# A hybrid decoder layer on one core: the fourth expert's down projection by column quarters, stores between them, and the last group of experts loaded in 4 MB transfers

## The chip, the cores and the metric

The kernel runs on one core of a Trainium2 chip. The metric is the device time of one execution in microseconds (us), the median of several. A profiled execution gives the trace from which the rows below come; its span runs from the first to the last instruction.

## What is computed

One step of one decoder layer, in fp32, for a prompt of 256 tokens and 8 sample tokens (264 rows of width 2048). First the mixer (differential attention and a short convolution side by side); then the part that this change touches, a mixture of 32 SwiGLU experts in 4 routing groups:

```python
def expert_block(args):
    xblk, e = args
    return (jax.nn.silu(xblk @ w_gate[e]) * (xblk @ w_up[e])) @ w_down[e]
...
xp = xp + hier_moe(rms_norm(xp, norm_ffn[l]), ...)   # top 1 group, top 2 experts in it
```

Each of the three matrices of an expert is 2048 x 512 or 512 x 2048 in fp32: 4 MB. All 32 experts are read, 96 matrices or 403 MB. Outputs are y_prompt (256 x 2048), y_sample (8 x 2048) and the keys, values and convolution states.

## The kernel before

**Stages.** Up to some 530 us the mixer and the router run. Then follow the experts, in 8 groups (NG) of 4 (EG). An expert has 32 slots (C) for tokens; 4 experts make up the 128 columns of a selection matrix.

**Names.** g, u and d with a digit are the gate, up and down matrix of an expert in a group (0 to 3). A matrix fills two of the 8 slots of `ring`, 2 MB each (a unit). SP issues all weight transfers in the order of LOADS: g0 u0 g1 u1 d0 g2 u2 d1 g3 u3 d2 d3. A transfer is issued once the unit that it overwrites has been used (`expert_used`). Groups 1 to 6 are loaded by `pairs`, one 4 MB transfer for a matrix; the first and the last group in units of 2 MB (line 539), the very last unit in two halves of 1 MB (lines 610 and 611).

**TensorE, expert by expert.** `gather` picks an expert's tokens, `turn_rows` turns them; `unit_products` (line 981) multiply them with g and u, four matmuls of 32 columns side by side, each giving a quarter of the contraction; `fold` adds the four parts up. `turn_hidden` turns the hidden rows and `down` (line 1018) multiplies them with d. `down` works through the contraction (4 chunks c, two in a unit) and in each chunk through the 4 column quarters n, which accumulate side by side in the 4 strips of 32 rows of bank 2. ScalarE copies bank 2 to `ye`: row strip n holds the expert's 32 slots for columns 512n to 512n+511. Software order puts `down` of expert j - 1 behind the products of expert j, and `mix` of expert j - 2 in between.

**Mix.** `turn_gate` (line 1049) turns the gate matrix (tokens x slots) into `gateT`, four times, one copy in each strip of 32 partitions. `mix` then multiplies 32 rows of `gateT` with 32 rows of `ye`, for each quarter n and row block t: t = 0 and 1 are the prompt's two blocks of 128 tokens, t = 2 the 8 sample tokens (line 1033, a 32x32 tile; the others line 1036). VectorE adds the result from its bank to `xa` (lines 1830 and 1824).

**The group's end.** Behind the products of the fourth expert (j = 3): four products `residual` (line 1055) load `xa[:, 1]` into banks 0, 1, 3 and 4, on which `mix_row` (line 1060) accumulates both last experts for row block 1; ScalarE moves the banks back to `xa` (line 1425). `mix_part` (line 1042) mixes the third expert for row block 0. Then gate 3 is turned, `down(3, 0)` and `down(3, 1)` run back to back, ScalarE copies `ye`, and the last expert is mixed: row block 0, row block 1, samples.

**Stores.** After the last group SP stores row block 0 in four transfers of 256 KB (line 624) and the samples in four of 16 KB (line 627), ScalarE's queue stores row block 1 in four of 256 KB (line 1437).

Of the kernel before, what the change touches and what calls it, by code (L numbers as in the profile page):

```python
# [15 lines left out]
ALU = mybir.AluOpType  # L16
# [103 lines left out]
STEPS = [(t, j) for j in range(EG - 2) for t in (0, 2, 1)] + [(t, j) for j in (EG - 2, EG - 1) for t in (0, 2)]  # L120
NSTEPS = len(STEPS) + 1
STEP_AT = {s: n + (n > STEPS.index((0, EG - 2))) for n, s in enumerate(STEPS)}
# [5 lines left out]
MIX_BANKS = {s: (4, 5, 6, 7) for s in STEPS}  # L128
MIX_BANKS.update({(2, j): (2,) for j in range(EG)})
MIX_BANKS[(0, EG - 2)] = (5, 7, 6, 5)  # L130
MIX_BANKS[(2, EG - 2)] = (7,)
MIX_BANKS[(0, EG - 1)] = (5, 6, 7, 2)
MIX_BANKS[(2, EG - 1)] = (5,)
ROW_BANKS = (0, 1, 3, 4)
GATE_BANK = (5, 5, 5, 6)
# [27 lines left out]
def build(nc, ins, outs):  # L163
    ctx = ExitStack()
    with ctx:
# [107 lines left out]
        gateT = bc[:, y0 + 2816:y0 + 3200].rearrange("p (t s) -> p t s", t=TT)  # L273
        g_sb = bc[:, y0 + 3200:y0 + 3712]
# [159 lines left out]
        end_in = sem("end_in")  # L434
# [5 lines left out]
        row_mixed = sem("row_mixed")  # L440
# [41 lines left out]
        def _(sp):  # L482
# [67 lines left out]
            def pairs(g, it):  # L550

                for n in range(UPG // 2):
                    kind, j = LOADS[n]
                    s = slot_of(NFRONT + TURN + 2 * n)
                    if 2 * n < SLOTS:
                        expert_used(2 * n + 1 - SLOTS + UPG, it - 1)
                    else:
                        expert_used(2 * n + 1 - SLOTS, it)
                    src = {"g": wg, "u": wu, "d": wd}[kind][bass.ds(g, 1), :, j, :].rearrange("o p n -> p (o n)")
                    sp.dma_start(ring[:, s:s + 2, :].rearrange("p a n -> p (a n)"), src).then_inc(slot_full[s], 16)  # L560
                    sp.sem_inc(slot_full[s + 1], 16)
                sp.sem_inc(end_in, 16)
# [25 lines left out]
            sp.sem_inc(end_in, 16)  # L588
# [10 lines left out]
            with sp.Else():  # L599
                for m in range(UPG):  # L600
                    s = slot_of(NFRONT + TURN + m)
                    if m < SLOTS:
                        expert_used(m - SLOTS + UPG, NG - 2)
                    else:
                        expert_used(m - SLOTS, NG - 1)
# [7 lines left out]
            y = outs["y_prompt"].rearrange("o (t p) d -> (o t) p d", p=P)  # L613
            every = npass * (NG * NADDS)
            last = EG - 1

            def added(step, n):

                sp.wait_ge(mix_added, every + (ADDS_BY[step] + n))

            for n in range(4):
                added((0, last), n - 3)
                cols = slice(512 * n, 512 * n + 512)
                sp.dma_start(y[0][:, cols], xa[:, 0, cols]).then_inc(y_stored, 16)
            added((2, last), 0)
            for n in range(4):
                sp.dma_start(outs["y_sample"].rearrange("b o d -> b (o d)")[:, n * 512:(n + 1) * 512],
                             xa[n * C:n * C + NB, 2, 0:512]).then_inc(y_stored, 16)
            sp.wait_ge(y_stored, 192)
# [6 lines left out]
        def _(pe):  # L636
# [265 lines left out]
            def gather(j, it):  # L902

                if j == 0:
                    pe.wait_ge(sel_ready, it + 5)
                elif j == 1:
                    pe.wait_ge(sel_ready, it + 4)
                    pe.wait_ge(mix_added, it * NADDS + NADDS)
# [42 lines left out]
            def experts(it, first):  # L951
# [49 lines left out]
                def down(j, i, hidden_of=None):  # L1001
# [9 lines left out]
                    for c in range(FC // 2):  # L1011
                        if (j, i, c) == (EG - 1, 1, 1):
                            pe.wait_ge(end_in, it * 16 + 16)
# [25 lines left out]
                def mix_part(step, n):  # L1039

                    rows_ = slice(n * C, (n + 1) * C)
                    return pe.matmul(bank[MIX_BANKS[step][n]][:, :], gateT[rows_, step[0], :], ye[rows_, :], start=True, stop=True)

                def turn_gate(j):

                    to = bank[GATE_BANK[j]]
# [6 lines left out]
                def residual(n):  # L1053

                    pe.matmul(bank[ROW_BANKS[n]][:, :], ident, xa[:, 1, n * 512:(n + 1) * 512], start=True, stop=False)  # L1055

                def mix_row(j, n):

                    rows_ = slice(n * C, (n + 1) * C)
                    m = pe.matmul(bank[ROW_BANKS[n]][:, :], gateT[rows_, 1, :], ye[rows_, :], start=False, stop=j == EG - 1)  # L1060
                    if j == EG - 1:
                        m.then_inc(row_mixed, 1)

                def next_rows(j):

                    if j == 0:
                        pe.wait_ge(mix_added, it * NADDS + NADDS)
                        pe.wait_ge(row_moved, it * 4 + 4)
                    gather((j + 1) % EG, it)

                for j in range(EG):
# [3 lines left out]
                    if j == 0:  # L1075
                        pe.wait_ge(row_moved, it * 4 + 2)
# [6 lines left out]
                    else:  # L1083
# [4 lines left out]
                        else:  # L1088
                            pe.wait_ge(ye_copied, e - 1)
# [33 lines left out]
                    if j == EG - 1:  # L1123
                        residual(2)
                    down(j - 1, 1)

                e = it * EG + EG - 1
                pe.wait_ge(xe_ready, 2 * e + 4)
                pe.wait_ge(ye_copied, e)
                pe.wait_ge(gateT_copied, e)  # L1130
                mix_part((0, EG - 2), 0)
                mix_part((0, EG - 2), 1)
                pe.wait_ge(act_ready, e + 1)
                mix_part((0, EG - 2), 2).then_inc(mixed, 1)
                for n in range(4):
                    mix_row(EG - 2, n)
                adds_done((0, EG - 2), -2)
                mix_part((0, EG - 2), 3).then_inc(mixed, 1)
                mix((2, EG - 2))
                adds_done((0, EG - 2), -1)  # L1140
                turn_gate(EG - 1)
                down(EG - 1, 0)
                down(EG - 1, 1)
                pe.wait_ge(ye_copied, e + 1)
                pe.wait_ge(gateT_copied, e + 1)
                adds_done((2, EG - 2))
                mix((0, EG - 1))
                for n in range(4):
                    if n == 3:
                        adds_done((0, EG - 1), -3)  # L1150
                    mix_row(EG - 1, n)
                mix((2, EG - 1))
# [9 lines left out]
        def _(act):  # L1162
# [228 lines left out]
            def experts(it, first):  # L1391

                def copy_gate(e, j):

                    act.wait_ge(gate_T, e + 1)
                    A(gateT, bank[GATE_BANK[j]][:, 0:TT * P].rearrange("p (t s) -> p t s", t=TT), ACT.Copy).then_inc(gateT_copied, 1)
# [6 lines left out]
                for j in range(EG):  # L1403
# [8 lines left out]
                    if j == 0:  # L1412
                        copy_gate(e, j)
                        continue
                    copy_ye(e - 1)
# [5 lines left out]
                copy_gate(it * EG + EG - 1, EG - 1)  # L1421
                copy_ye(it * EG + EG - 1)
                for n in range(4):
                    act.wait_ge(row_mixed, it * 4 + (n + 1))
                    A(xa[:, 1, n * 512:(n + 1) * 512], bank[ROW_BANKS[n]][:, :], ACT.Copy).then_inc(row_moved, 1)
# [8 lines left out]
            for n in range(4):  # L1434
                cols = slice(512 * n, 512 * n + 512)
                act.wait_ge(row_moved, npass * (NG * 4) + (n + 1))
                act.dma_start(y[1][:, cols], xa[:, 1, cols]).then_inc(y_stored, 16)
# [3 lines left out]
        def _(dve):  # L1441
# [343 lines left out]
            V.memset(esum[:, 2:3], 0.0).then_inc(row_moved, 4)  # L1785
# [14 lines left out]
            with dve.Fori(0, npass) as r:  # L1800
                with dve.Fori(0, NG) as g:
# [16 lines left out]
                    def mix_adds(step):  # L1818
# [7 lines left out]
                        for n in range(4):  # L1826
                            if step == (0, EG - 2) and n == 3:
                                dve.wait_ge(mixed, it * NSTEPS + (NSTEPS + STEP_AT[step] + 2))
# [3 lines left out]
                    for j in range(EG):  # L1832
# [5 lines left out]
                        if j >= 2:  # L1838
                            for t in (0, 2, 1):
                                if (t, j) == (1, 2):  # L1840
                                    dve.wait_ge(row_moved, it * 4 + 4)
# [10 lines left out]
                    for t in (0, 2):  # L1852
                        mix_adds((t, EG - 2))
                    for t in (0, 2):
                        mix_adds((t, EG - 1))
# [109 lines left out]
```

## Time and profile before

| | us |
|---|---|
| median of 3 runs | 1441.41 (1439.46 to 1441.7) |
| profiled execution, its own time | 1440.47 |
| its span, first to last instruction | 1438.6 |
| TensorE busy | 1256.8 (87%) |
| VectorE busy | 450.5 (31%) |
| ScalarE busy | 223.1 (16%) |
| moved by DMA | 503.61 MB, mean 350 GB/s |
| mean granted TensorE clock | 0.959 |

The profiled execution's own time lies 1.9 us above its span. Busy shares are averages over stages with different limits; only waits in a stage tell what sets its pace. A row of the form `[5.01 <-DMA x]` says that the engine stood 5.01 us before this instruction and that the DMA x ended the wait. An fp32 matmul appears as two instructions (x2). Four matmuls that run side by side in strips overlap, so that their group's busy time is short.

### The profile page before, as it was taken

The page shows a single profiled execution, that of the slowest core. Times are in us where ns is not written, and L with a number is a line of the kernel's source. Part 1 is how long each engine was busy: PE and PEld are TensorE (multiplying, and loading weights), DVE is VectorE, ACT ScalarE, POOL GpSimd, SP SyncE. Part 2 cuts the span into 40 slices and gives each one's busy share as a digit, 9 for nine tenths or more (in the row PEclk, how much of TensorE's full clock was granted, in tenths as well). Part 3 has the DMA queues.
Part 4 walks back from the last instruction along what each step waited for, and adds up shares of the span by engine and source line. Part 5 has one row for each costly group of instructions (what it writes and reads, how often), then busy time and mean ns, then how long its engine had stood idle before and what let it go on. Part 6 is the DMA issues. An engine that isn't in the chain of part 4 may idle for free.

```text
span 1438.6 us, 19986 instructions
## 1 busy us (share of the span) xinstructions
PE 1256.8 (87%) x8413; PEld 650.3 (45%) x8413; DVE 450.5 (31%) x887; ACT 223.1 (16%) x465; POOL 44.8 (3%) x30
## 2 busy tenths in 40 slices
PE   8999999999999998997787777887788777778777
PEld 7888888888788862231222222222222122222222
DVE  4322127674211142332321321331232232233142
ACT  3111232322000033110011011011001001111101
POOL 0000003140000001000000000000000000000000
PEclk9999999999999999999998999899899999999899
DMA  9975443669399349999999999999999999999997
GB/s 342 348 222 183 141 132 121 207 203 340 89 349 409 119 164 428 417 428 430 433 428 436 427 433 436 427 434 431 430 436 427 433 436 426 436 428 426 430 429 308
DMA packets 101729, 503.61 MB, mean 350 GB/s; under 512 B 9470, under 2 KB 79750, under 8 KB 85302
## 3 DMA queue, kind: packets, MB, share of 16 engines
q1 hardware_dynamic: 89618, 494.37, 84.6%
q10 hardware_dynamic: 12068, 8.63, 1.9%
q8 instruction: 32, 0.52, 0.1%
q14 instruction: 11, 0.09, 0.0%
HBM read 496.42 MB, written 6.59 MB: 350 GB/s over the span
## 4 chain that ended last, share of the span: by engine, by line
PE 55%; DMA 41%; DVE 2%; ACT 1%; issue 1%; SPq 1%; ACTq 0%; DVEq 0%
PE bank L702 30%; DMA ring<-in_w_gate 16%; DMA ring<-in_w_up 14%; DMA ring<-in_w_down 10%; PE bank L981 9%; PE bank L1018 4%; PE bank L916 2%; PE bank L1036 2%; DMA ring<-in_w_in 1%; PE bank L1033 1%; PE bank L1055 1%; DVE xa L1830 1%; PE bank L1049 1%; PE bank L998 0%; PE bank L793 0%
## 5 line engine op out<-in xcount | busy, mean ns | idle before, releaser
L702 PE MATMUL bank<-bc,ring 128*128 128x264 f32 x1536 | 350.9, 387 | 1.9 <-ACT cat L1186 1.3
L981 PE MATMUL bank<-ring,bc 128*32 128x512 f32 x2040 | 268.2, 659 | 89.5 <-DMA ring<-in_w_gate 58.5
L702 PEld LDWEIGHTS bank<-bc,ring 128*128 128x128 f32 x1536 | 288.1, 190 | 52.4 <-issue 2.3
L1830 DVE TENSOR_TENSOR xa<-xa,bank 128x512 f32<-128x512 f32 x192 | 119.8, 682 | 243.5 <-PE bank L1036 196.0
L981 PEld LDWEIGHTS bank<-ring,bc 128*32 128x32 f32 x2040 | 63.2, 117 | 264.5 <-issue 153.4
L702 PE MATMUL bank<-cat,ring 128*128 128x264 f32 x512 | 116.0, 387 | 0.0
L702 PEld LDWEIGHTS bank<-cat,ring 128*128 128x128 f32 x512 | 96.6, 190 | 19.0 <-issue 2.9
L1844 DVE COPY bc<-bank 128x512 f32<-128x512 f32 x32 | 22.1, 691 | 210.3 <-PE bank L981 210.3
L1018 PE MATMUL bank<-ring,cat 128*32 128x512 f32 x480 | 66.4, 674 | 19.9 <-DMA ring<-in_w_down 19.7
L916 PE MATMUL bank<-cat,bc 128*32 128x512 f32 x512 | 61.3, 597 | 13.5 <-DVE xa L1830 13.5
L1018 PE MATMUL bank<-ring,xa 128*32 128x512 f32 x512 | 62.3, 607 | 6.3 <-DMA ring<-in_w_down 4.1
L1406 ACT ACTIVATE bc<-bank 128x512 f32<-128x512 f32 x32 | 19.1, 596 | 264.4 <-PE bank L981 264.4
L1036 PE MATMUL bank<-bc 32*128 32x512 f32 x320 | 51.5, 716 | 8.0 <-ACT bc L1401 6.3
L1498 DVE RECIPROCAL xa<-xa 128x264 f32<-128x264 f32 x16 | 28.8, 1803 | 85.2 <-ACT xa L1236 85.2
L991 PE MATMUL bank<-bc,consts 128*32 128x512 f32 x64 | 32.8, 593 | 21.7 <-DVE bc L1844 21.7
L1401 ACT ACTIVATE bc<-bank 128x512 f32<-128x512 f32 x32 | 19.1, 597 | 195.8 <-PE bank L1018 195.8
L1875 POOL TENSOR_TENSOR ring<-ring 128x1024 f32<-128x1024 f32 x16 | 37.6, 2376 | 285.1 <-DVE xa L1547 285.1
L1765 DVE TENSOR_TENSOR bc<-bank,gains 128x512 f32<-128x512 f32 x32 | 22.1, 692 | 74.4 <-PE bank L923 74.4
L1018 PEld LDWEIGHTS bank<-ring,cat 128*32 128x32 f32 x480 | 13.4, 117 | 56.0 <-issue 35.3
L1373 ACT ACTIVATE bc<-bank 128x512 f32<-128x512 f32 x32 | 19.1, 597 | 124.5 <-PE bank L916 124.5
L1678 DVE TENSOR_TENSOR bc<-bc,bank 128x264 f32<-128x264 f32 x16 | 6.9, 429 | 99.4 <-PE bank L702 99.4
L1036 PEld LDWEIGHTS bank<-bc 32*128 32x128 f32 x320 | 14.4, 211 | 51.7 <-issue 34.9
(286 smaller groups left out, 981.9 us busy)
## 6 DMA issues: line engine op xcount, KB each, us to landing
ring<-in_w_gate SPq DMA_DIRECT2D x24, 4096.0 KB, 31.2
ring<-in_w_up SPq DMA_DIRECT2D x24, 4096.0 KB, 31.3
ring<-in_w_down SPq DMA_DIRECT2D x24, 4096.0 KB, 32.6
ring<-in_w_in SPq DMA_DIRECT2D x23, 2048.0 KB, 13.9
ring<-in_w_up SPq DMA_DIRECT2D x16, 2048.0 KB, 22.9
ring<-in_w_gate SPq DMA_DIRECT2D x15, 2048.0 KB, 28.9
ring<-in_w_down SPq DMA_DIRECT2D x13, 2048.0 KB, 28.7
ring<-in_w_out SPq DMA_DIRECT2D x8, 2048.0 KB, 16.5
```

What stands on the lines that cost most here:

```text
L702: m = pe.matmul(bank[n % 3][:, 0:T], w[:, k, (i % TPU) * P:(i % TPU + 1) * P], src[:, k, :], start=n_k == 0, stop=n_k == KT - 1)
L916: m = pe.matmul(bank[4][c * C:(c + 1) * C, :], lhs, rhs, start=t == 0, stop=t == TT - 1, skip_group_check=True)
L981: m = pe.matmul(bank[b][c * C:(c + 1) * C, :], xeT[j % 2][:, k, :], wx, start=i == 0 and x < 4, stop=i == 1 and x >= 4, skip_group_check=True)
L991: pe.matmul(bank[3][0:C, :], const("fold"), g_sb, start=True, stop=True, skip_group_check=True)
L1018: m = pe.matmul(bank[2][n * C:(n + 1) * C, :], actT[j % 2][:, i * FC // 2 + c, :], wc[:, n * 512:(n + 1) * 512], start=i == 0 and c == 0, ...
L1036: m = pe.matmul(bank[to[n]][:, :], gateT[rows_, t, :], ye[rows_, :], start=True, stop=True)
L1373: A(xrow, bank[4][:, :], ACT.Copy).then_inc(xrow_copied, 1)
L1498: st.do(V.reciprocal(r, r))
L1765: V.tensor_tensor(xeT[j % 2].rearrange("p (m c) s -> p m c s", m=4), bank[7][:, :].rearrange("p (m c s) -> p m c s", m=4, c=4), gffn.rearr ...
L1830: V.tensor_tensor(xa[:, t, cols], xa[:, t, cols], bank[to[n]][:, :], ALU.add).then_inc(mix_added, 1)
L1844: V.tensor_copy(u_sb, bank[1][:, :]).then_inc(u_copied, 1)
L1875: G.tensor_tensor(kp, kp, ring[:, sq_, (b % 4) * ATT:(b % 4 + 1) * ATT], ALU.mult).then_inc(page_mul, 1)
```

## The change

1. In the last group each matrix is one 4 MB transfer. The last one, d3, comes in three: columns 0 to 1023 of all chunks (2 MB), then quarters 2 and 3 (1 MB each), with a semaphore of their own.
2. In all groups the fourth expert's `down` goes by column quarters: `end_products(q)` runs the 4 contraction chunks of quarter q side by side in the strips of bank 2, each a part sum. ScalarE copies the bank to `g_sb` or `u_sb` in turn.
3. The sum over the chunks is left to the mix: `mix_last(q)` multiplies all 128 rows of a gate matrix of its own, `gateT3` (four equal copies of the gates), with the 128 rows of part sums. It accumulates on what `mix_second_last` put into the same bank for the third expert.
4. Gate 3 is turned before `down(2)` instead of before `down(3)`; three of the four `residual` products go, one stays, for quarter 3 of row block 1. VectorE does the other adds of row block 1.
5. The stores go by column quarter: row blocks 0 and 1 together (512 KB) and the samples for quarters 0 to 2, each as soon as its adds are done; for quarter 3 samples and row block 0 on SP, row block 1 on ScalarE's queue.

```diff
+END_STEPS = [(t, q) for q in range(3) for t in (0, 1, 2)] + [(t, 3) for t in (2, 0, 1)]
+END_BANKS = {0: (5, 0, 3, 5), 1: (7, 1, 4, 7), 2: (6, 6, 6, 6)}
...
-                for m in range(UPG):
-                    s = slot_of(NFRONT + TURN + m)
...
-                    if m < UPG - 1:
-                        stream_unit(NG - 1, m, s)
-                        continue
-                    src = source(NG - 1, m)
-                    sp.dma_start(ring[:, s, 0:UNIT // 2], src[:, 0:UNIT // 2]).then_inc(slot_full[s], 16)
-                    sp.dma_start(ring[:, s, UNIT // 2:], src[:, UNIT // 2:]).then_inc(end_in, 16)
+                for n in range(UPG // 2):
+                    kind, j = LOADS[n]
+                    s = slot_of(NFRONT + TURN + 2 * n)
...
+                    if n < UPG // 2 - 1:
+                        src = {"g": wg, "u": wu, "d": wd}[kind][NG - 1, :, j, :]
+                        sp.dma_start(ring[:, s:s + 2, :].rearrange("p a n -> p (a n)"), src).then_inc(slot_full[s], 16)
+                        sp.sem_inc(slot_full[s + 1], 16)
+                        continue
+                    src = wd[NG - 1, :, EG - 1, :].rearrange("p (c d) -> p c d", c=FC)
+                    to = ring[:, s:s + 2, :].rearrange("p a (c d) -> p (a c) d", c=FC // 2)
+                    sp.dma_start(to[:, :, 0:1024], src[:, :, 0:1024]).then_inc(slot_full[s], 16)
+                    sp.sem_inc(slot_full[s + 1], 16)
+                    for q in (2, 3):
+                        cols = slice(512 * q, 512 * q + 512)
+                        sp.dma_start(to[:, :, cols], src[:, :, cols]).then_inc(end_in[q - 2], 16)
...
+            for q in range(3):
+                cols = slice(512 * q, 512 * q + 512)
+                sp.wait_ge(end_added, every + END_ADD[(1, q)])
+                sp.dma_start(y[:, :, cols], xa[:, 0:2, cols]).then_inc(y_stored, 16)
+                sp.wait_ge(end_added, every + END_ADD[(2, q)])
+                sp.dma_start(ys[:, cols], xa[q * C:q * C + NB, 2, 0:512]).then_inc(y_stored, 16)
...
+                def mix_second_last(t, q):
+
+                    rows_ = slice(q * C, (q + 1) * C)
+                    pe.matmul(bank[END_BANKS[t][q]][:, :], gateT[rows_, t, :], ye[rows_, :],
+                              start=(t, q) != (1, 3), stop=False, skip_group_check=True)
+
+                def end_products(q):
+
+                    if q == 0:
+                        pe.wait_ge(ye_copied, it * (EG - 1) + EG - 1)
...
+                    else:
+                        pe.wait_ge(end_copied, it * 4 + q)
+                    if q >= 2:
+                        pe.wait_ge(end_in[q - 2], it * 16 + 16)
+                    for c in range(FC):
+                        m = pe.matmul(bank[2][c * C:(c + 1) * C, :], actT[(EG - 1) % 2][:, c, :],
+                                      end_weights[c // 2][:, c % 2, q * 512:(q + 1) * 512], start=True, stop=True, skip_group_check=True)
...
+                def mix_last(q):
+
+                    pe.wait_ge(end_copied, it * 4 + q + 1)
+                    for t, q_ in END_STEPS:
+                        if q_ != q:
+                            continue
+                        if t == 2:
+                            m = pe.matmul(bank[END_BANKS[2][q]][q * C:(q + 1) * C, :], gateT3[:, 2, 0:C], (g_sb, u_sb)[q % 2],
+                                          start=False, stop=True, skip_group_check=True)
+                        else:
+                            m = pe.matmul(bank[END_BANKS[t][q]][:, :], gateT3[:, t, :], (g_sb, u_sb)[q % 2],
+                                          start=False, stop=True, skip_group_check=True)
+                        m.then_inc(end_mixed, 1)
...
                     if j == EG - 1:
-                        residual(0)
-                        residual(1)
-                        residual(3)
+                        pe.wait_ge(gateT_copied, e)
+                        turn_gate(EG - 1)
...
-                    if j == EG - 1:
-                        residual(2)
                     down(j - 1, 1)
...
+                pe.wait_ge(act_ready, e + 1)
+                end_products(0)
...
+                for t in (0, 1):
+                    for q in range(3):
+                        mix_second_last(t, q)
+                for q in range(4):
...
+                end_products(1)
+                mix_last(0)
+                end_products(2)
+                mix_last(1)
...
+                pe.matmul(bank[END_BANKS[1][3]][:, :], ident, xa[:, 1, 1536:2048], start=True, stop=False, skip_group_check=True)
+                mix_second_last(1, 3)
+                mix_second_last(0, 3)
+                end_products(3)
+                mix_last(2)
+                mix_last(3)
```

## Rows read from the trace of the kernel before

**Rows 1.** The page: 40 slices of TensorE and DMA rate, and the chain by engine.
```profile
PE   8999999999999998997787777887788777778777
...
GB/s 342 348 222 183 141 132 121 207 203 340 89 349 409 119 164 428 417 428 430 433 428 436 427 433 436 427 434 431 430 436 427 433 436 426 436 428 426 430 429 308
...
PE 55%; DMA 41%; DVE 2%; ACT 1%; issue 1%; SPq 1%; ACTq 0%; DVEq 0%
```

**Rows 2.** Windows: length, busy us (instructions) by engine, granted clock, DMA share, GB/s.
```profile
12.00:30.00 18.00, 16.11 (x72) 13.35 (x73) 8.93 (x30) 5.37 (x11) 0.00 (x0) 1.00 1.07 366
...
700.00:1300.00 600.00, 477.16 (x3772) 137.87 (x3765) 163.76 (x312) 69.94 (x124) 0.00 (x0) 0.93 1.00 432
1310.00:1418.00 108.00, 89.37 (x714) 25.46 (x714) 29.98 (x58) 12.94 (x23) 0.00 (x0) 0.94 1.01 429
...
1424.00:1426.00 2.00, 2.00 (x32) 0.74 (x25) 0.23 (x1) 0.49 (x1) 0.00 (x0) 1.00 0.11 45
```

**Rows 3.** Issue to landing: all of line 560 (4 MB), then line 611 (last megabyte).
```profile
DMA to landing us min/median/max: 21.8/31.4/35.1
...
L611 SPq DMA_DIRECT2D ring<-in_w_down x1: 433/433/433, 1389.8 to 1389.8; - x1
...
DMA to landing us min/median/max: 35.5/35.5/35.5
```

**Rows 4.** Timeline of TensorE, groups 1, 5, 6, 7: first products with g3, first L1042.
```profile
695.78 3.64 PE L981 MATMUL bank<-ring,bc 128*32 128x512 f32 x16 [5.15 <-DMA ring<-in_w_gate]
...
724.30 0.70 PE L1042 MATMUL bank<-bc 32*128 32x512 f32 x3 [0.76 <-issue]
...
1162.08 3.27 PE L981 MATMUL bank<-ring,bc 128*32 128x512 f32 x16 [5.07 <-DMA ring<-in_w_gate]
...
1278.65 3.64 PE L981 MATMUL bank<-ring,bc 128*32 128x512 f32 x16 [5.01 <-DMA ring<-in_w_gate]
...
1307.51 0.70 PE L1042 MATMUL bank<-bc 32*128 32x512 f32 x3 [0.76 <-issue]
...
1395.99 1.92 PE L981 MATMUL bank<-ring,bc 128*32 128x512 f32 x16 [1.00 <-DMA ring<-in_w_gate]
...
1418.85 0.70 PE L1042 MATMUL bank<-bc 32*128 32x512 f32 x3 [0.76 <-issue]
```

**Rows 5.** Windows: the first products with g3 in group 6.
```profile
1278.60:1282.30 3.70, 3.65 (x20) 0.68 (x20) 0.00 (x0) 0.00 (x0) 0.00 (x0) 0.50 1.00 427
```

**Rows 6.** The chain that ended last, from 1410 us: start, us, what.
```profile
1410.15 2.58 PE bank L1055 x6
...
1415.17 1.06 PE bank L1055 x2
1416.23 1.85 PE bank L1018 x16
1418.08 0.76 issue
...
1422.49 0.99 PE bank L1033 x8
1423.48 0.79 PE bank L1049 x24
...
1427.77 0.60 ACT bc L1401
...
1428.50 1.14 PE bank L1036 x8
...
1432.62 0.69 DVE xa L1824
```

**Rows 7.** The stores: SP's issues (timeline), and the window in which bytes begin.
```profile
1430.41 2.13 SPq L624 DMA_DIRECT2D out_y_prompt<-xa  x4
...
1433.34 3.28 SPq L627 DMA_DIRECT2D out_y_sample<-xa  x4
...
1431.00:1431.50 0.50, 0.50 (x4) 0.01 (x2) 0.50 (x1) 0.50 (x3) 0.00 (x0) 1.00 0.46 176
```

More of the change, by code:

```diff
@@ L115 @@
 SLOPES = [2.0 ** (-8.0 * (h + 1) / H) for h in range(H)]
[L120 to L122 removed]
+STEPS = [(t, j) for j in range(EG - 2) for t in (0, 2, 1)]
+NSTEPS = len(STEPS)
+STEP_AT = {s: n for n, s in enumerate(STEPS)}
 ADDS_BY, _n = {}, 0
@@ L433, in build @@
         half_used = sem("half_used")
-        end_in = sem("end_in")
+        end_in = [sem(f"end_in{i}") for i in range(2)]
         down_half = sem("down_half")
@@ L613, in _ @@
[L613 to L628, printed above, removed]
@@ L630, in _ @@
+            cols = slice(1536, 2048)
+            sp.wait_ge(end_added, every + END_ADD[(2, 3)])
+            sp.dma_start(ys[:, cols], xa[3 * C:3 * C + NB, 2, 0:512]).then_inc(y_stored, 16)
+            sp.wait_ge(end_added, every + END_ADD[(0, 3)])
+            sp.dma_start(y[:, 0, cols], xa[:, 0, cols]).then_inc(y_stored, 16)
+            sp.wait_ge(y_stored, 144)
             sp.wait_ge(state_stored, 16)
@@ L1037, in mix @@
                     m.then_inc(mixed, 1)
-                def mix_part(step, n):
-                    rows_ = slice(n * C, (n + 1) * C)
-                    return pe.matmul(bank[MIX_BANKS[step][n]][:, :], gateT[rows_, step[0], :], ye[rows_, :], start=True, stop=True)
                 def turn_gate(j):
-                    to = bank[GATE_BANK[j]]
+                    to = bank[5]
                     for t in range(TT):
@@ L1414, in experts @@
                         continue
+                    if j == EG - 1:
+                        copy_gate(e, j)
                     copy_ye(e - 1)
@@ L1420, in experts @@
                               ).then_inc(x0_ready, 1)
[L1421 to L1425, printed above, removed]
+                for q in range(4):
+                    if q < 3:
+                        act.wait_ge(end_down, it * 3 + q + 1)
+                    else:
+                        act.wait_ge(down_done, it * EG + EG)
+                    if q >= 2:
+                        act.wait_ge(end_mixed, it * len(END_MIX) + 3 * (q - 1))
+                    A((g_sb, u_sb)[q % 2], bank[2][:, :], ACT.Copy).then_inc(end_copied, 1)
+                act.wait_ge(end_mixed, it * len(END_MIX) + END_MIX[(1, 3)])
+                A(xa[:, 1, 1536:2048], bank[END_BANKS[1][3]][:, :], ACT.Copy).then_inc(row_moved, 1)
             experts(0, True)
@@ L1433, in _ @@
             y = outs["y_prompt"].rearrange("o (t p) d -> (o t) p d", p=P)
[L1434 to L1437, printed above, removed]
+            act.wait_ge(row_moved, npass * NG + 1)
+            act.dma_start(y[1][:, 1536:2048], xa[:, 1, 1536:2048]).then_inc(y_stored, 16)
         @block.vector
@@ L1851, in _ @@
                             select(0, P, False)
[L1852 to L1855, printed above, removed]
+                    for t, q in END_ADD:
+                        dve.wait_ge(end_mixed, it * len(END_MIX) + END_MIX[(t, q)])
+                        rows_ = slice(q * C, (q + 1) * C) if t == 2 else slice(0, P)
+                        cols = slice(0, 512) if t == 2 else slice(q * 512, (q + 1) * 512)
+                        V.tensor_tensor(xa[rows_, t, cols], xa[rows_, t, cols], bank[END_BANKS[t][q]][rows_, :], ALU.add
+                                        ).then_inc(end_added, 1)
             assert st.n - before == LOOP_STEPS, st.n - before
```

97 lines of the change are left out of this document (39 added, 58 removed).

## The prediction

> **What bounds the kernel now.** I read the 40 slices first. From 540 us to the last slice the DMA moves 417 to 436 GB/s, in all but one 426 or more, while TensorE is busy seven or eight tenths in most slices [rows 1]. The chain gives TensorE 55% and the DMA 41% of the whole, but in the expert stage what TensorE waits for last is a weight transfer. So two questions decide: does the stream stay full, and what stands between the last weights and the end?
>
> The stream: 432 GB/s from 700 to 1300 us, where each transfer is 4 MB and the DMA engines' busy share is 1.00, and 429 GB/s from 1310 to 1418 us, where the last group comes in 2 MB [rows 2]. Issues land 31.4 us later in the median, 21.8 at least [rows 3]. One 4 MB transfer takes 9.71 us of the stream: TensorE starts on the fourth expert's gate matrix ("g3") the moment it lands, at 1162.08 and 1278.65 us, 116.57 us or 12 transfers apart, and at 695.78 four groups before 1162.08 (116.58 us each) [rows 4]. So at issue there are always 12 us or more of other bytes queued ahead. That is the cover of everything that TensorE does later in groups 0 to 6.
>
> The end: the last megabyte is issued at 1389.8 and landed 35.5 us later, 1425.3 us [rows 3]; bytes have nearly stopped in 1424 to 1426 us [rows 2]. TensorE isn't waiting for it: it is still at the group's tail, a chain without a gap above 0.8 us from 1410 to the end of the last mix at 1432.6 us [rows 6]. Then come one add (0.69 us), four stores of the sample rows that hold SP for 3.28 us, and 2.0 us from the last issue (1436.6) to the end, 1438.6 us [rows 6, 7]. So the end is set by TensorE's chain behind the gate and up matrices of the fourth expert, and 6.0 us of adds and stores behind it.
>
> **Part 1: 4 MB transfers in the last group.** Gain: with 12 transfers in the group's rhythm g3 is whole at 1278.60 + 116.57 = 1395.2 us, where its second half now lands at 1396.0 [rows 4]; 0.8 us. Loss: now its first half is there at 1391.0, and TensorE does eight products, two mixes and their adds before the second half comes; the first mix of the third expert (L1042) starts at 1418.85, 22.9 us after the second half [rows 4]. With a whole pair, groups 1 to 6 show the same work: 28.5, 28.3, 27.8, 27.8, 27.5 and 28.9 us from g3's arrival to that mix, mean 28.1 (the first and the last of the six are shown) [rows 4]. The long ones are those in which the first 16 instructions after 5 us of idling took 3.64 us, where at 1395.99, after 1 us of waiting, they took 1.92: the granted clock was 0.50 in that stretch [rows 5], the level of 1.2 GHz, after TensorE had stood for 5 us. I take 28.1: the mix would start at 1395.2 + 28.1 = 1423.3 us instead of 1418.85. This costs 4.4 us, the biggest term. The issues themselves wait for the later half of what they overwrite, some microseconds more; they have 12 us of queue ahead and cost nothing. The other weights keep pace: u3 at 1404.9 and d2 at 1414.6 us, against a first `down` of expert 2 at 1415.3 below.
>
> **Part 2: residual products and the gate transposes moved.** The four products that put row block 1 into the banks go (2.58 + 1.06 us), and the transposes of gate 3 come to their place (0.79 us) [rows 6]: -2.85 us. They cover the wait for the hidden product less than the residuals did; 0.79 us just reach it, a miss costs some 0.1 to 0.4 us. So the fourth expert's first quarter can start at 1423.3 - 2.85 = 1420.4 us. Its wait for `ye` is the same 0.76 us as now [rows 6].
>
> **Part 3: the last matrix in pieces.** It would land whole at 1395.2 + 3 x 9.71 = 1424.3 us, its first two column quarters 4.9 us sooner, 1419.4. Pieces are 4 KB and 2 KB instead of 8 KB and more. The nearest row is the window 12 to 30 us with w_in's 1 KB pieces: 366 GB/s against 432 [rows 2], so 2.87 us instead of 2.43 for a megabyte of 1024 pieces, 0.43 ns a piece. 512 pieces of 4 KB and 1024 of 2 KB cost 0.7 us together: first half 1419.6, last 1425.0 us. Bounds: 0 and twice that. The Trainium skill (DMA: Bandwidth & Descriptors, Specifications) says that pieces of 512 B or more run at line rate; by that the 0.7 us are nothing, the row speaks against it, and the sum is the same either way. For TensorE is at quarter 0 at 1420.4, and at quarter 3 only ten microseconds later: the landing no longer sets anything, by 0.8 us at the first quarter.
>
> **Part 4: the new tail on TensorE.** The unit is one round of the array with 512 columns in fp32, 0.86 us: L1055's three full matmuls take 2.58 us; four matmuls of 32 columns or of 32 rows side by side take the same round plus a change of tiling: L1018 1.85 for two rounds (+0.13), L1033 0.99 (+0.13), L1036 1.14 (+0.28), a single full one 1.06 (+0.20) [rows 6]. No row has a 128-row, 32-column matmul alone; it can't be under a round, and at most two of them share one.
> - `end_products`, 4 calls: 4 rounds, as many as `down` had.
> - `mix_second_last` for quarters 0 to 2: 2 rounds; both of quarter 3 use the same 32 rows: 2 rounds.
> - the sample rows' second-last mixes: 1 round.
> - `mix_last`: row blocks 0 and 1 take a full matmul for each quarter: 8 rounds. Now they are 1.14 us for four.
> - sample rows: 4 matmuls of 32 columns, the last two side by side: 3 rounds.
> - one residual product: 1 round.
>
> 21 rounds are 18.1 us. Changes of tiling: six to 32-column form at 0.13, two to 32-row form at 0.28, one to 32x32 at 0.13, five to full at 0.20: 2.5 us. Sum 20.5 us; bounds 18.1 (no change costs anything) and 21.4 (the last two sample mixes one by one). The Trainium skill (TensorEngine Tiling, Key Properties) has the rule that speaks against this change: switching the tiling form drains the engine. It names no price; the trace agrees with 0.13 to 0.28 us where the form changes and 0.00 within L1055's three. Without the rule the sum would be 2.5 us less.
>
> Every other wait in the tail is covered: ScalarE's copy of a quarter (0.60 us [rows 6]) lies under 1 to 3 rounds, VectorE's 11 adds (0.69 each) come one for each round. TensorE ends at 1420.4 + 20.5 = 1440.9 us, now 1432.6.
>
> **Part 5: the stores.** Now 6.0 us from TensorE's end. The last product is (row block 1, quarter 3); behind it ScalarE's copy 0.6, its issue 0.4, 2.0 from the last issue to the end as now [rows 7], 256 KB more to move at 379 GB/s or so 0.7, and 0.2 of hops: 3.9 us. The six stores of quarters 0 to 2 have gone under the tail. Bounds 3.1 (the first store's bytes begin 0.9 us after its issue [rows 7], so part of the 2.0 may be shared) and 4.9 (the quarter-2 store of 512 KB and two sample stores of 0.8 us each on SP still ahead).
>
> **Part 6: groups 0 to 6.** The same tail there, some 4 us longer, and d3's slots free about 5 us later, since TensorE must await d3 whole (1307.7 us in group 6) before the first quarter. Behind it are only queue entries with 12 us of other bytes ahead [rows 3], and TensorE, however late its tail, stands 5 us before g3 of the next group [rows 4]. Nothing, and the full price of a dry queue if 12 us weren't enough.
>
> **Sum.** 1440.9 + 3.9 = 1444.8 us of span, against 1438.6: +6.2 (4.4 from Part 1, -2.85 from Part 2, +6.7 for the tail (20.5 against 13.8 from 1418.85 to 1432.6), -2.1 from the stores). The profiled execution took 1440.47 us for its span of 1438.6, 0.9 under the median. 1440.5 + 6.2 = 1446.7 and 1441.4 + 6.2 = 1447.6; I forecast 1447.0.
>
> **Rivals.**
> *A, as summed* (0.60): 1447.0, its own range 1444.5 to 1449.5.
> *B, not slower by what can be told* (0.17): the new tail packs better than counted. For: matmuls of 32 rows and 32 columns overlap in these rows down to one round for four, and the sample mixes and the next `end_products` have the same form. If three sample rounds vanish and half the changes cost nothing, the tail is 20.5 - 2.6 - 1.2 = 16.7 us, and the time 1443.2. It decides from 3.3 us saved on (0.2% is 2.9). Against: in each pair one 32-column strip is shared, and full products lie between.
> *C, faster* (0.07): the full mixes take one pass of 0.43 instead of two. 8 x 0.43 = 3.4 saved wouldn't do; it needs every round of the tail near half: 1437.5. L1055's rows, same form and type, speak against it.
> *D, slower still* (0.12): after the 6 us wait for g3 the lower clock lasts longer, or the stores queue: 1450.
> *E* (0.04): a dry queue in the middle groups, 2 us for each of seven groups or more: 1455 or beyond.
>
> If Part 1 doesn't bite (full clock after g3's wait), the landing at 1419.6 us is next, so it gives back only 0.8 us; that stays in A.
>
> **Range and chances.** A measurement of this kernel can tell about 0.2% (2.9 us) from no change. The range goes from B's lower side, 1441.5, to D, 1450.5. Slower: A, D, E and none of B, 0.76; within 0.2%: B, 0.17; faster 0.07.
>
> **What would show it.** In the profile after: g3 in group 7 waited for until 1395.2 and first `end_products` near 1420.4; no DMA wait at quarters 1 to 3; full mixes of 0.86 us each in `mix_last`; TensorE's last product near 1441; the ACT-queue store as the last thing, some 4 us behind it; 432 GB/s unchanged from 700 to 1300 us. The prediction is wrong if the tail from first quarter to last product is under 17 us, or if g3's chain takes under 25 us.

## The result, and the profile after

The changed kernel takes 1447.24 us in the median of six executions, the kernel before, measured with it, 1440.77: ratio 1.0039 (95% interval 1.0028 to 1.005), so it is slower. One of the six took 2173.69 us at a mean granted clock of 0.553; the ratio leaves it out, and the median of the other five is 1446.86 us, 6.1 us over the kernel before. The forecast was 1447.0. The profiled execution took 1447.63 us for a span of 1445.5.

The page after: DMA rate in 40 slices and the chain by engine.

```profile
GB/s 342 348 223 181 136 131 124 216 192 345 100 347 388 117 196 428 394 434 432 429 428 435 433 431 428 434 435 429 428 434 435 430 429 433 435 430 431 431 434 228
...
PE 65%; DMA 30%; DVE 2%; ACT 1%; issue 1%; SPq 1%; ACTq 0%; DVEq 0%
```

The stream is as full as before from the eighteenth slice on; the 17th lost 23 GB/s, and the last is emptier, since more work stands behind the last weights. TensorE has 10 points more of the chain. Most of them lie in the middle groups, where the chain now meets mainly the down matrices (25% of the span; before it was gate 16%, up 14%, down 10%). In the last group the chain leaves the DMA for good at g3's landing (1396.3 us), where before it left it at u3's (1405.6), which is some 9 us. Windows, columns as in [rows 2]: the middle of the stage, then the first products with g3 in the last group.

```profile
700.00:1300.00 600.00, 496.54 (x3758) 142.88 (x3761) 168.67 (x316) 71.56 (x124) 0.00 (x0) 0.93 1.00 432
...
1396.30:1400.00 3.70, 3.70 (x20) 0.72 (x20) 0.00 (x0) 0.00 (x0) 0.00 (x0) 0.50 1.01 434
```

432 GB/s, unchanged, though TensorE works 19 us more in the 600: the longer tails of groups 0 to 6 are hidden. The answers to [rows 3]: issue to landing of all of line 562 (the 4 MB transfers in the loop), then the first half of d3 and its quarter 3.

```profile
DMA to landing us min/median/max: 17.9/31.1/34.3
...
DMA to landing us min/median/max: 29.7/29.7/29.7
...
L622 SPq DMA_DIRECT2D ring<-in_w_down x1: 17689/17689/17689, 1392.5 to 1392.5; - x1
...
DMA to landing us min/median/max: 33.6/33.6/33.6
```

The shortest time to landing fell from 21.8 to 17.9 us, about what the group's end grew by (6.7 us of tail less 2.85 before it); with 9.7 us for a transfer's own bytes, 8 us of queue are left. The first half of d3 was issued at 1391.1 and landed at 1420.8, quarter 3 at 1426.1. TensorE's chain through the last group (start, us, what):

```profile
1396.30 3.64 PE bank L990 x16
...
1421.05 0.61 ACT bc L1424
1421.65 0.04 issue
1421.70 1.06 PE bank L1071 x8
1422.76 1.92 PE bank L1058 x12
1424.68 0.99 PE bank L1162 x8
1425.67 1.00 PE bank L1071 x8
1426.67 1.91 PE bank L1087 x4
1428.58 0.55 PE bank L1084
1429.13 0.03 PE bank L1071 x3
1429.16 0.40 PE bank L1084
1429.56 0.86 PE bank L1071 x5
...
1433.31 1.05 PE bank L1169 x2
1434.36 1.91 PE bank L1058 x4
1436.28 0.99 PE bank L1071 x8
...
1439.18 0.98 PE bank L1084 x4
1440.17 1.93 PE bank L1087 x4
```

L1071 is `end_products`, L1058 `mix_second_last`, L1087 the full `mix_last`, L1084 its 32-column form, L1169 the residual product. From the first quarter at 1421.70 to the end of the last product at 1442.10 TensorE doesn't wait once. Two full matmuls take 1.91 us each time: two rounds of 0.86 and 0.2 for the change of tiling. At 1428.58 the sample mix and the next `end_products` are interleaved, and four strips with five matmuls take two rounds. Behind it, timeline of the last stores:

```profile
1441.63 0.29 SPq L635 DMA_DIRECT2D out_y_sample<-xa  x1
1442.12 0.60 ACT L1455 ACTIVATE xa<-bank 128x512 f32<-128x512 f32 x1 [4.08 <-PE bank L1087]
1442.35 0.36 SPq L637 DMA_DIRECT2D out_y_prompt<-xa  x1
1442.74 0.37 ACTq L1465 DMA_DIRECT2D out_y_prompt<-xa  x1
```

The last store is issued 0.6 us after the last product, and the span ends 2.4 us after that issue ends: 3.4 us from TensorE's end, where it was 6.0.

### The profile page after: what moved, and what is told of

The parts are those of the page before. It is cut to its first block, busy times and chain, and to the rows that moved or that the text cites. A ratio compares the mean times of both kernels' runs of the same rounds, so it can differ in the third digit from the quotient of the medians.

```text
span 1445.5 us, 20006 instructions
## 1 busy us (share of the span) xinstructions
PE 1292.9 (89%) x8365; PEld 658.6 (46%) x8365; DVE 459.6 (32%) x896; ACT 225.7 (16%) x465; POOL 44.8 (3%) x30
## 4 chain that ended last, share of the span: by engine, by line
PE 65%; DMA 30%; DVE 2%; ACT 1%; issue 1%; SPq 1%; ACTq 0%; DVEq 0%
PE bank L711 30%; DMA ring<-in_w_down 25%; PE bank L990 9%; DMA ring<-in_w_gate 4%; PE bank L1087 4%; PE bank L925 4%; PE bank L1025 3%; PE bank L1058 3%; PE bank L1071 3%; PE bank L1084 2%; DMA ring<-in_w_in 1%; PE bank L1000 1%; PE bank L1162 1%; PE bank L1007 1%; PE bank L1169 1%
## 5 line engine op out<-in xcount | busy, mean ns | idle before, releaser
L990 PE MATMUL bank<-ring,bc 128*32 128x512 f32 x2040 | 253.4, 631 | 62.7 <-DMA ring<-in_w_gate 60.9
L1857 DVE TENSOR_TENSOR xa<-xa,bank 128x512 f32<-128x512 f32 x128 | 79.4, 682 | 149.0 <-PE bank L1043 142.7
L1883 DVE TENSOR_TENSOR xa<-xa,bank 128x512 f32<-128x512 f32 (+1 forms) x88 | 60.4, 686 | 164.5 <-PE bank L1087 157.1
L1071 PE MATMUL bank<-ring,xa 128*32 128x512 f32 x256 | 46.7, 702 | 29.6 <-DMA ring<-in_w_down 28.1
L1025 PE MATMUL bank<-ring,cat 128*32 128x512 f32 x480 | 59.5, 599 | 4.5 <-DVE bc L1874 2.9
L1087 PE MATMUL bank<-bc,xa 128*128 128x512 f32 x128 | 63.5, 618 | 0.0
L1429 ACT ACTIVATE bc<-bank 128x512 f32<-128x512 f32 x32 | 19.1, 596 | 221.5 <-PE bank L990 221.5
L1453 ACT ACTIVATE bc<-bank 128x512 f32<-128x512 f32 x32 | 19.1, 597 | 153.9 <-PE bank L1071 153.9
L1043 PE MATMUL bank<-bc 32*128 32x512 f32 x256 | 40.8, 710 | 1.7 <-DVE xa L1857 1.7
L1025 PE MATMUL bank<-ring,xa 128*32 128x512 f32 x256 | 33.3, 627 | 9.2 <-DMA ring<-in_w_down 8.4
L1087 PEld LDWEIGHTS bank<-bc,xa 128*128 128x128 f32 x128 | 21.7, 189 | 43.2 <-issue 43.2
```

Source lines behind the costliest of these rows:

```text
L990: m = pe.matmul(bank[b][c * C:(c + 1) * C, :], xeT[j % 2][:, k, :], wx, start=i == 0 and x < 4, stop=i == 1 and x >= 4, skip_group_check=True)
L1025: m = pe.matmul(bank[2][n * C:(n + 1) * C, :], actT[j % 2][:, i * FC // 2 + c, :], wc[:, n * 512:(n + 1) * 512], start=i == 0 and c == 0, ...
L1043: m = pe.matmul(bank[to[n]][:, :], gateT[rows_, t, :], ye[rows_, :], start=True, stop=True)
L1071: m = pe.matmul(bank[2][c * C:(c + 1) * C, :], actT[(EG - 1) % 2][:, c, :], end_weights[c // 2][:, c % 2, q * 512:(q + 1) * 512], start=Tr ...
L1087: m = pe.matmul(bank[END_BANKS[t][q]][:, :], gateT3[:, t, :], (g_sb, u_sb)[q % 2], start=False, stop=True, skip_group_check=True)
L1857: V.tensor_tensor(xa[:, t, cols], xa[:, t, cols], bank[to[n]][:, :], ALU.add).then_inc(mix_added, 1)
```

## The experiments

Theory: three terms make the time. (1) A pair that lands whole delays the chain behind g3. (2) The last expert's tail is TensorE work, round by round. (3) Stores between take bytes from the end. Rival: only one of them counts and the others are hidden. Each kernel was timed in alternation with the kernel before; the ratio is to that.

**The changed kernel again.** 

> The changed kernel once more, for comparison on the same chip: 6.4 us over the kernel before. If the first group's short gap in the weight stream (1.1 us more than in the profile of before) belongs to the change and not to one execution, it is there again at 580 to 585 us.

1446.41 us, 1.0039 (1.0025 to 1.0052). The gap in the stream was there too. Where it comes from is below.

**Term 1 alone.**

```diff
-                for m in range(UPG):
+                for n in range(11):
+                    kind, j = LOADS[n]
...
+                    sp.dma_start(ring[:, s:s + 2, :].rearrange("p a n -> p (a n)"), src).then_inc(slot_full[s], 16)
+                    sp.sem_inc(slot_full[s + 1], 16)
+                for m in range(22, UPG):
```

> The kernel before with only its last group's loads changed: g0 to d2 in 4 MB transfers, d3 as before. Theory (the products with g3 now begin when the whole pair has landed): g3 at 1395.2, the first mix of the third expert 27.5 to 28.9 us later at 1423.3 instead of 1418.85, the tail of 13.8 us and the 6.0 us behind it unchanged: +4.4 us. Rival (the pair costs nothing, the longer tail of the changed kernel is all of its loss): within 0.5 us of the kernel before.

1445.26 us, ratio 1.0032 (1.002 to 1.0044), span 1443.3: +4.7 over 1438.6. TensorE, timeline:

```profile
1395.57 2.93 PE L991 MATMUL bank<-ring,bc 128*32 128x512 f32 x16 [3.80 <-DMA ring<-in_w_gate]
...
1423.39 0.70 PE L1052 MATMUL bank<-bc 32*128 32x512 f32 x3 [0.76 <-issue]
```

The first mix of the third expert starts at 1423.39, 27.8 us after g3 landed, against 1418.85 in [rows 4]; the rest of the chain is unchanged. The rival falls: two thirds of the loss (4.7 of 6.9 us of span) come with a change of loads that saves the stream 0.7 to 0.8 us.

**Pairs only where TensorE doesn't need halves.** The same edit with `range(8)` (g0 to d1) and `range(16, UPG)`.

> The kernel before with g0 to d1 of the last group in 4 MB transfers, g3 to d3 in 2 MB units as before; nothing else. Theory (a 4 MB transfer takes 9.71 us of the stream, two of 2 MB 9.80; only pairs that TensorE works through unit by unit at the end must stay apart): all landings from g3 on 0.7 us sooner, and the chain behind them too: 0.7 us under the kernel before. Rival (pairs delay the chain wherever they are): slower, as before_4mb was by 4.6 us.

1440.56 us, 0.9994 (0.9985 to 1.0003). In the profile the last product ends at 1431.7, the span at 1437.7, 0.9 under the kernel before, of which the stream was 0.35 ahead already in group 6 (g3 landed there at 1278.26 for 1278.61). The pairs are left with 0.6 us of the 0.7 expected. So the mechanism is there in the profile; the timing can't tell it from nothing.

**Term 1 undone in the changed kernel.**

```diff
+                    if 8 <= n < UPG // 2 - 1:
+                        for i in range(2):
+                            stream_unit(NG - 1, 2 * n + i, s + i)
+                        continue
```

> The changed kernel with g3, u3 and d2 of the last group in units of 2 MB again, all else kept. Theory: TensorE reaches the first quarter of the fourth expert's down about 5 us sooner, at 1416.3, but the first half of d3 lands only at 1420.8, and it has to wait for that: 0.85 us less than the changed kernel, with a wait of some 4 us before the first quarter. Rival (the terms add up whatever the landing): 4.4 us less.

1448.35 us, 1.0055 (1.0041 to 1.0069): about 2 us over the changed kernel, which neither expected. The two intervals overlap, so the time alone doesn't show it slower; it does show that the 4.4 us of the rival aren't gained. What follows rests on the profile, in which the stream was 2.2 us ahead of the changed kernel's in group 6. The timeline of TensorE, and the window of the first quarter:

```profile
1413.86 1.92 PE L1029 MATMUL bank<-ring,cat 128*32 128x512 f32 x16 [2.20 <-DMA ring<-in_w_down]
...
1419.08 1.93 PE L1075 MATMUL bank<-ring,xa 128*32 128x512 f32 x8 [3.30 <-DMA ring<-in_w_down]
1420.94 3.79 PE L1062 MATMUL bank<-bc 32*128 32x512 f32 x12
1424.67 1.50 PE L1166 MATMUL bank<-bc 32*32 32x512 f32 x8
```
```profile
1419.00:1422.00 3.00, 2.92 (x14) 0.78 (x17) 0.00 (x0) 0.60 (x1) 0.00 (x0) 0.50 1.02 375
```

TensorE did wait for d3, as forecast. Behind the wait of 2.20 us its products still took 1.92 us, but behind the one of 3.30 us the granted clock was 0.50, and the tail began with two groups at nearly twice their time (1.93 for 1.06, 3.79 for 1.99) and a third at 1.50 for 1.06. From first quarter to last product it took 23.5 us, not 20.4.

**The same, TensorE kept at work in the two waits.**

```diff
+                    if j == EG - 1:
+                        for _ in range(7):
+                            pe.matmul(bank[2][:, 0:P], ident, ident, start=True, stop=True)
...
+                for _ in range(9):
+                    pe.matmul(bank[7][:, 0:P], ident, ident, start=True, stop=True)
```

The edit does this in every group, not only in the last.

> The kernel of after_units with idle TensorE kept at work: 7 matmuls of 128x128 (0.25 us each) before the fourth expert's down(2, 0) and 9 before its first quarter; their results are never read. after_units came out 1.9 us slower than the changed kernel where 0.85 us faster was expected: it waited 2.2 us for d2 and 3.3 us for d3, as the theory had it, but the next three groups then ran at the lower clock (1.93, 3.72 and 1.43 us where the changed kernel has 1.06, 1.92 and 0.99). Theory: without those 3.1 us it is 0.85 us faster than the changed kernel, 1445.6 us. Rival (it is the 2 MB transfers that cost, through a slower stream or a later landing of d3): no change against after_units, 1448.4.

1448.29 us, 1.0052 (1.0039 to 1.0066). In the profile the theory's part is there: the waits are 0.48 and 1.10 us, the first groups take 1.06, 1.92 and 0.99, first quarter 1422.36 to last product 1442.76 are 20.4 us. Measured from the landing of g3's second half (1397.4), the last product ends 45.4 us later; in after_units 48.4 (1394.2 to 1442.6), in the changed kernel 45.8 from the pair's landing. The time shows none of the 3 us. In the two profiles the stream accounts for that: it was 1.0 us behind the changed kernel's in group 6 and 3.2 behind after_units'. Of these 3.2 us 0.3 were there at 556 us. Some 1.8 came in group 0, where the gather took 3.50 us and in after_units 1.92 (see the last section). A further 1.1 were lost between 716 and 746 us, in two transfers of 10.0 and 10.5 us with 33 us from issue to landing, so not for lack of issues. Single transfers of 9.9 to 11.3 us at 676 to 746 us, issued 30 us or more ahead, stand in six of the thirteen traces, that of the kernel before among them. What delays them, and whether the runs that were not profiled had the same losses, is open: the time doesn't confirm the theory.

**The wait before g3 filled instead.** 18 such matmuls into bank 0 before the products with g3 of every group, in the changed kernel.

> The changed kernel with 18 matmuls of 128x128 (0.25 us each, never read) in the wait of 5.3 us before the products with g3, so that TensorE stays at its higher clock. Theory: those products take 1.92 instead of 3.64 us and the mixes after them 0.4 us less, 2.1 us in all; then d3's first half, landed at 1420.8, is the next wait, and 0.7 us are left: 0.7 us under the changed kernel. Rival (d3's landing has slack): 2.1 us under it.

1447.33 us, 1.0044 (1.0031 to 1.0058): in time not told from the changed kernel. TensorE, timeline:

```profile
1395.79 1.92 PE L990 MATMUL bank<-ring,bc 128*32 128x512 f32 x16 [1.03 <-DMA ring<-in_w_gate]
...
1415.31 1.92 PE L1025 MATMUL bank<-ring,cat 128*32 128x512 f32 x16 [1.25 <-DMA ring<-in_w_down]
```

1.92 instead of 3.64 us, and from g3's landing to the last product 45.2 instead of 45.8 us: 0.6 of 2.1 us left, as expected, though it was d2 that came next, with 1.25 us, and not d3: that had landed 0.2 us before TensorE came to it.

**d3 not cut by columns.**

```diff
+                        pe.wait_ge(end_in[0], it * 16 + 16)
+                        pe.wait_ge(end_in[1], it * 16 + 16)
                         end_weights[:] = [weights("d", EG - 1, i).rearrange("p (c d) -> p c d", c=FC // 2) for i in range(2)]
```

> The changed kernel, but the first quarter of the fourth expert's down waits for all of d3, both late quarters too, as it would have to if d3 came in whole rows. Theory: the wait ends at about 1426.1 instead of 1421.7, +4.4 us; and TensorE stands 5 us before it, so that what follows runs at the lower clock as in after_units, up to +3.1 us: between 4.4 and 7.5 us more than the changed kernel, 1451 to 1454. Rival (the landing of d3 is hidden, its cut by columns is worth nothing): no change.

1454.98 us, 1.01 (1.0084 to 1.0115), about 8 us over the changed kernel.

```profile
1424.52 1.94 PE L1073 MATMUL bank<-ring,xa 128*32 128x512 f32 x8 [5.53 <-DMA ring<-in_w_down]
```
```profile
1424.50:1430.00 5.50, 5.48 (x20) 1.42 (x20) 0.00 (x0) 0.60 (x1) 0.00 (x0) 0.50 0.00 0
```

The tail starts 29.9 us after g3's products do, not 25.4, and takes 24.2 us (to 1448.7), not 20.4; its first 5.5 us are at a granted clock of 0.50. The lower clock cost 3.8 us where 3.1 was the most expected, so the time lies a little above the range given. The cut by columns is worth both; the rival falls.

**Term 2, the sample mixes shortened.** This kernel leaves out most of the last expert's part of y_sample.

```diff
-                            m = pe.matmul(bank[END_BANKS[2][q]][q * C:(q + 1) * C, :], gateT3[:, 2, 0:C], (g_sb, u_sb)[q % 2],
+                            m = pe.matmul(bank[END_BANKS[2][q]][q * C:(q + 1) * C, 0:64], gateT3[:, 2, 0:C], (g_sb, u_sb)[q % 2][:, 0:64],
```

> The changed kernel with the last expert's mix of the sample rows cut to 64 of 512 columns (448 columns of each quarter of y_sample lack that expert). Theory (every round of the tail lies on the path to the end): three rounds of 0.86 us shrink to some 0.11, 2.2 us less than the changed kernel; groups 0 to 6 don't count. Rival (the sample mixes run beside the products of the same form, or the stores set the end): under 0.8 us less.

1445.31 us, 1.0029 (1.0017 to 1.004), span 1443.5. First quarter 1421.57 to last product 1439.71:

```profile
1437.50 0.30 PE L1084 MATMUL bank<-bc,xa 128*32 128x64 f32 x4
1437.73 1.98 PE L1087 MATMUL bank<-bc,xa 128*128 128x512 f32 x4
1438.32 0.39 SPq L630 DMA_DIRECT2D out_y_prompt<-xa  x1
1439.04 0.30 SPq L632 DMA_DIRECT2D out_y_sample<-xa  x1
1439.75 0.60 ACT L1455 ACTIVATE xa<-bank 128x512 f32<-128x512 f32 x1 [3.33 <-PE bank L1087]
```

18.1 us, 2.3 less than 20.4: the sample mixes are three rounds on the path and don't hide. Behind the last product 0.4 us of it are lost again (3.8 us to the end instead of 3.4); the time, 1.1 us under the changed kernel run again, is within what can be told.

**Term 3 undone.** In the changed kernel all of SP's stores wait for `END_ADD[(0, 3)]`.

> The changed kernel with all stores of SP held back until the last add (row block 0, quarter 3). Theory (a store costs its bytes: 2.1 MB at 371 GB/s are 5.7 us, and the end is the last byte): the first byte 0.9 us after the issue at 1442.4, 5.7 us of bytes, 1.0 us to the end: 1450.0 of span, 4.5 us more than the changed kernel. Rival (what counts behind TensorE is the number of issues on SP, the bytes are hidden): eight issues of 0.3 to 0.4 us, 1.5 us more.

1451.55 us, 1.0069 (1.0056 to 1.0083). SP's issues, and the window of the bytes:

```profile
1443.21 0.41 SPq L630 DMA_DIRECT2D out_y_prompt<-xa  x1
...
1448.86 0.36 SPq L636 DMA_DIRECT2D out_y_prompt<-xa  x1
```
```profile
1444.00:1449.00 5.00, 0.00 (x0) 0.00 (x0) 0.00 (x0) 0.00 (x0) 0.00 (x0) 0.70 0.99 358
```

The last product ended at 1442.95 and the span at 1451.3: 8.35 us instead of 3.4, 4.9 more. From 1444 to 1449 us the DMA is busy at 358 GB/s. At the end bytes count, 2.1 MB of them with ScalarE's store; the rival, 1.5 us, falls.

**Looking for a faster kernel: gaps of TensorE.** In the kernel before `residual(0)` goes ahead of `fold`, `residual(2)` behind `down(2, 1)`.

```diff
+                    if j == EG - 1:
+                        pe.wait_ge(g_copied, e + 1)
+                        residual(0)
                     fold(e)
...
-                        residual(0)
                         residual(1)
                         residual(3)
```

With g0 to d1 in 4 MB: 

> The kernel before with two residual products moved into gaps of TensorE at the group's end (residual(0) before the fold, where it stands 0.86 us; residual(2) behind down(2, 1), where it stands 0.76 us), and g0 to d1 of the last group in 4 MB transfers, g3 to d3 in 2 MB as before. Theory: the gaps give 0.7 and 0.7 us, eight 4 MB transfers 0.09 us each over 2 MB ones, 0.7 us; sum 2.1 us less than the kernel before, 1438.8 us, if the last megabyte, at 1424.6, stays ahead of the last quarter of down. Rival (the gaps are waits that move along): 0.7 us less at most.

1440.17 us, 0.9991 (0.9982 to 1.0): 1.1 us under the kernel before, where 2.1 were expected, and not told from nothing. A new wait stands in the profile:

```profile
1415.90 1.92 PE L1028 MATMUL bank<-ring,cat 128*32 128x512 f32 x16 [1.18 <-DMA ring<-in_w_down]
```

Without the change of loads: 

> The kernel before with the two residual products moved into TensorE's gaps, no change of loads. before_gaps_4mb gained 1.1 us where 2.1 were expected: it waited 1.18 us for d2's second half before down(2, 1). If the landing of d2 is what ate the rest, the gaps alone, with d2 landing at 1415.4 instead of 1414.7, are worth 0.3 us; if the gaps are worth their 1.4 us, the time is 1.4 us under the kernel before.

1440.42 us, 0.9991 (0.9982 to 1.0). A wait of 1.19 us for d2 stands at the same place, and the last product ends 0.3 us later than before with a stream 0.7 us later: 0.4 us gained. So of the 1.4 us of the gaps 0.4 are left; the landing of d2 takes the place of the rest. These two are the fastest kernels here, but neither can be told from the kernel before.

## Why the prediction was right, step by step

- **Part 1, g3.** Predicted whole at 1395.2, products at once; they began at 1396.30. The 1.1 us are the stream's: in group 6 it was already 1.1 us behind (g3's landing at 1279.7 for 1278.6). The gain by 4 MB transfers was there: 116.6 us from one g3 to the next. Counted between TensorE's starts, as in the prediction, it is 0.8 us; between landings it is 0.7, since g3's second half had landed at 1395.85, 0.14 us before TensorE took it up.
- **Parts 1 and 2, g3 to first quarter.** Predicted 25.2 us (28.1 - 2.85), measured 25.4. before_4mb shows the 4.4 us as +4.5 for the first mix. The lower clock was in it, as in the groups that the number was read from; after_g3_busy took it out and gained 0.6 us in the profile, where the prediction had said that 0.8 would come back.
- **Part 3, d3.** First half predicted at 1419.6, landed at 1420.8, the last at 1426.1 for 1425.0: again the 1.1 us of the stream. The pieces of 4 and 2 KB do cost: the matrix took 10.4 us of the stream against 9.71, the 0.7 us that were priced (2 MB in 4 KB pieces 5.1 us against 4.9, the two megabytes in 2 KB pieces 2.7 and 2.6 against 2.5). That it fits so well is partly luck: the window from which the price was read also moved hundreds of pieces under 1 KB. That this sets nothing held: no wait at quarters 0 to 3. That its slack at quarter 0 is small held too: it was 0.9 us, 0.2 us were left in after_g3_busy, and after_units waited 3.3 us.
- **Part 4, the tail.** 20.5 predicted, 20.4 measured; full pairs 1.91 for 1.92, side-by-side groups 0.99 to 1.06, and the sum of rounds was confirmed by taking three of them out (2.3 us). No row before had shown a 128-row, 32-column matmul alone; it took 0.98 us with its change, one round.
- **Part 5, the stores.** 3.9 predicted, 3.4 measured. Too large by 0.5 us: behind the copy and the issue, which were as taken, came 2.4 us to the end, where I had 2.0 and 0.7 for bytes, and next to nothing for the 0.2 of hops. The lower bound was 3.1.
- **Part 6, groups 0 to 6.** The tail there is hidden, as predicted. But the sentence that at issue there are always 12 us queued ahead is wrong for group 0: u2's second half, issued at 580.1, landed 7.2 us later, so nothing lay ahead of it. That didn't come from this change, but it let 1.1 us in that no term had.
- Rival B (the tail packs better) and D (worse) both stayed away, since form changes and rounds were what the rows said. Rival C is excluded by the 1.91 us of the full pairs.
- Not shown: no run has the new tail with all the loads of the kernel before. The 6.7 us of the tail rest on its trace and on the run that took three rounds out.

In the profile the terms add to 1396.3 + 25.4 + 20.4 + 3.4 = 1445.5 us. The errors are +1.1 for the stream, +0.2, -0.1 and -0.5; that 1446.86 us lies within 0.2 us of 1447.0 owes something to their signs. The first belongs to the profiled execution and not to the change: it comes from the clock in one stretch of group 0, as the last section shows. That execution took 1447.63 us, 2.1 us over its span where the prediction had taken 1.9 from the kernel before; whether the others had the same stretch no run shows. So the agreement to a few tenths is luck, that of the terms of 25 and 20 us isn't.

## What to carry to other kernels

A tail is priced by counting the array's rounds: four products that ran side by side in 32-row strips and become full-height ones cost four rounds instead of one, and the cut of the data by columns doesn't give that back here: it only keeps the landing of the last matrix from adding some 8 us. Merging two transfers saves the stream little (here 0.08 us for 4 MB) and makes the first half of the data as late as the second; merge where the consumer is behind, not at the end. Before removing a wait or a delay, ask what is late next (here d2 and d3 within 1 us), and what the engine's clock does in the new wait.

## What the runs showed of the hardware beyond the prediction

**The clock can turn a gained wait into a loss.** In after_d3_whole TensorE stood 5.53 us and then worked 5.5 us at the granted clock 0.50; its tail took 3.8 us more than 20.4. In after_units it stood 2.20 and 3.30 us; the products behind the first wait ran at a granted clock of 1.00, the three groups behind the second took 3.1 us more in sum, and so did its tail. With both waits filled (after_units_busy) the tail was 20.4 us again.

**One drop of the clock moves everything behind it.** In group 0 the gather at 575 us took 3.41 us in the changed kernel and 1.92 in the kernel before. TensorE's timeline, then the clock window of after:

```profile
575.07 3.41 PE L925 MATMUL bank<-cat,bc 128*32 128x512 f32 x16 [0.81 <-DVE xa L1857]
```
```profile
575.00:578.40 3.40, 3.33 (x16) 0.59 (x16) 1.80 (x4) 0.00 (x0) 0.00 (x0) 0.54 0.96 407
```

Right behind it SP waits for TensorE to free a slot while the queue is empty, so the 1.3 us go straight into the stream and stay to the end. All thirteen traces bear this out. In eight the gather takes 1.92 or 1.93 us, and SP issues u2's second half 4.83 us after the gather's start in every one. In five it takes 3.25 to 3.51 us (the changed kernel, the same again, before_4mb, before_gaps_4mb and after_units_busy), and the issue comes 6.15 to 6.47 us after the start. The work and the waits ahead of the gather (1.69 and 0.81 us) are the same in the kernel before and the changed kernel, so the drop belongs to an execution and not to the change: three of the eight kernels made from the changed one have it, and two of the five made from the kernel before. What decides it no run shows.

**A DMA issue can hold SP for 17.7 us.** The transfer of d3's quarter 3 in 2 KB pieces, issued at 1392.5 behind some 30 us of queue, kept SP until 1410.2 us. All eight kernels with this load show such an issue, of 13.7 to 18.6 us, while those of 4 MB ahead of it took 0.33. It cost nothing here, since SP's next work was at 1429.
